# Gated linear attention in a hybrid decoder layer: the output banks are multiplied by weight and gate first, and divided by the root later and in pieces

## What is computed

```
def _head_rms(x, g):                       # per head, 128 values
    y = xf * lax.rsqrt(jnp.mean(xf * xf, axis=-1, keepdims=True) + EPS)
    return y.reshape(...) * g

oa = _gla(qa, ka, va, log_a)               # 4 heads x 128 values, 512 tokens
ya = (_head_rms(oa, gla_norm) * silu(ga)) @ w_up_a
```

```
qk = silu(_causal_dwconv(concatenate([qc, kc]), mlstm_conv))
log_f = log_sigmoid(fc + mlstm_b_f)
```

## Time and profile before

| | us |
|---|---|
| median of 3 runs (lowest, highest) | 1457.63 (1456.39, 1460.25) |
| the profiled execution: its time | 1462.21 |
| its span, from the first to the last instruction | 1460.4 |
| TensorE busy in the span | 1334.4 (91%) |
| VectorE busy | 1038.5 (71%) |
| ScalarE busy | 778.6 (53%) |
| GpSimd busy | 432.5 (30%) |
| mean granted TensorE clock | 0.948 |

### The profile page before, as it was taken

The page is one execution under the profiler, slowest core; times in us unless marked ns, Lnnn a source line. Parts: engine busy times, 40 slices in busy tenths (PEclk is TensorE's granted clock), DMA queues, the critical chain, the costliest instruction groups (busy, mean ns, idle before and its releaser), DMA issues.

```text
span 1460.4 us, 19415 instructions
## 1 busy us (share of the span) xinstructions
PE 1334.4 (91%) x6398; PEld 1023.7 (70%) x6398; DVE 1038.5 (71%) x1302; ACT 778.6 (53%) x952; POOL 432.5 (30%) x321
## 2 busy tenths in 40 slices
PE   4897888998788979998997999999999999999986
PEld 2686678665445547887974888787788888888842
DVE  1538585375798645544467898888889999998927
ACT  3613332343233443222132888888788888888811
POOL 1100010002221000000001366665656666666610
PEclk8897989889898989999998999999999999999998
DMA  9233312103023505324134999999999999999856
GB/s 300 80 102 133 116 29 87 44 15 108 20 81 130 188 15 175 107 93 159 37 130 155 330 389 412 396 384 371 341 360 387 366 350 360 359 359 358 319 214 254
DMA packets 126617, 314.57 MB, mean 215 GB/s; under 512 B 24229, under 2 KB 61418, under 8 KB 118122
## 3 DMA queue, kind: packets, MB, share of 16 engines
q1 hardware_dynamic: 108282, 288.73, 54.6%
q0 software_dynamic: 18288, 25.21, 4.8%
HBM read 316.49 MB, written 38.80 MB: 243 GB/s over the span
## 4 chain that ended last, share of the span: by engine, by line
PE 62%; DMA 13%; DVE 13%; issue 5%; ACT 4%; POOL 2%; SPq 1%; POOLq 0%; DVEq 0%; ACTq 0%
PE bank L899 15%; PE bank L1285 9%; PE bank L1313 7%; PE bank L904 7%; DMA arena<-h_dram,tok_of 6%; PE bank L1289 5%; DMA ring<-in_exp_w_up 4%; PE bank L1272 3%; DVE arena L2071 2%; DVE top L2070 2%; DMA ring<-in_w_in 1%; PE bank L1354 1%; DMA arena<-in_ada_w 1%; PE bank L846 1%; PE bank L1142 1%
## 5 line engine op out<-in xcount | busy, mean ns | idle before, releaser
L2325 DVE TENSOR_TENSOR ring_parts<-ring,arena_parts 128x2048 fp32r<-128x2048 f32 x186 | 423.2, 2289 | 59.0 <-ACT arena_parts L1670 56.5
L1670 ACT ACTIVATE arena_parts<-ring 128x2048 fp32r<-128x2048 f32 x186 | 356.0, 1930 | 41.2 <-DMA ring<-in_exp_w_up 39.7
L1285 PE MATMUL bank<-arena_parts,oTA_parts 128*128 128x512 f32 x496 | 200.0, 403 | 2.7 <-DVE oTC_parts L2341 1.5
L1285 PE MATMUL bank<-arena_parts,oTC_parts 128*128 128x512 f32 x496 | 194.7, 393 | 0.0
L1313 PE MATMUL bank<-arena_parts,oTB_parts 128*128 128x512 f32 x496 | 161.3, 407 | 5.1 <-DVE ring_parts L2325 5.1
L899 PE MATMUL bank<-hT_parts,ring_parts 128*128 128x512 f32 x344 | 145.9, 424 | 7.4 <-ACT arena L1575 3.7
L794 POOL DMA_INDIRECT y_dram<-arena,row_of x62 | 96.3, 1553 | 176.9 <-ACT arena L1697 173.8
L769 POOL DMA_INDIRECT arena<-h_dram,tok_of x61 | 129.4, 2121 | 54.5 <-POOL tok_of L781 51.0
L899 PE MATMUL bank<-x_parts,ring_parts 128*128 128x512 f32 x344 | 139.1, 404 | 0.0
L1289 PE MATMUL bank<-ring_parts,oTA_parts 128*128 128x512 f32 x496 | 133.9, 392 | 0.0
L1397 ACT ACTIVATE ring_parts<-ring 128x2048 fp32r<-128x2048 f32 (+1 forms) x38 | 64.7, 1709 | 104.6 <-DMA ring<-in_w_in 57.3
(11 more groups left out here) (421 smaller groups left out, 2299.5 us busy)
## 6 DMA issues: line engine op xcount, KB each, us to landing
ring<-in_exp_w_gate SPq DMA_DIRECT2D x124, 512.0 KB
ring<-in_exp_w_up SPq DMA_DIRECT2D x124, 512.0 KB
ring<-in_exp_w_down SPq DMA_DIRECT2D x62, 1024.0 KB
ring<-in_w_in SPq DMA_DIRECT2D x25, 1024.0 KB, 5.4
ring<-in_ada_w SPq DMA_DIRECT2D x16, 1024.0 KB, 5.8
arena<-in_ada_w SPq DMA_DIRECT2D x4, 2048.0 KB, 16.8
x<-in_x SPq DMA_DIRECT2D x2, 2048.0 KB, 12.2
ring<-in_w_o SPq DMA_DIRECT2D x4, 1024.0 KB, 5.4
```

The lines of the kernel that those rows point to most:

```text
L1285: mm(out_gu, t[c][:, tile_cols(4 * k + j)], hi[:, :, j, :], start=(k == 0 and j == 0 and x_ == 0), stop=False)
L1670: A(w_hi[c][k], w_raw[c][k], ACT.Copy).then_inc(sem("gu_hi_ready" if k < 2 else "down_hi_ready"), 1)
L2325: v.tensor_tensor(w_lo[c][k], w_raw[c][k], w_hi[c][k].bitcast(F32), ALU.subtract).then_inc(sem("gu_lo_ready" if k < 2 else "down_lo_ready" ...
```

## The change

The product by norm weight and gate is made first, straight from the bank, and gives the bank back; the division by the root is made later, in place. The roots have four buffers of their own in oT[2] in place of two in the arena (the fourth is sqA's place). GpSimd's clearing waits for the four bank reads alone. ScalarE splits w_qkc1 after the first square and w_vc0 right after the four roots, which now stand together behind the squares. VectorE divides head 0 ahead of the three copies of mb, and heads 1 to 3 behind the values of branch C.

```diff
-        rsA = [ra.take(T) for _ in range(2)]
-        hA = ra.take(T)
+        rsA = [oT[2][:, h, :] for h in range(4)]
+        ra.at += 3 * T
...
-            pool.wait_ge(sem("oTA_ready"), 4)
-            pool.wait_ge(sem("mb_ready"), 3)
+            pool.wait_ge(sem("oA_read"), 4)
             g.memset(raw, 0.0)
...
             split_hi("w_qkc0")
-            split_hi("w_qkc1")
-            for h in range(5):
-                if h < 4:
-                    b = done(act, f"oA{h}")
-                    if h:
-                        b1 = done(act, f"msA{h - 1}")
-                        if h == 3:
-                            act.wait_ge(sem("oA_read"), 1)
-                        A(rsA[(h - 1) % 2], b1[:, :], ACT.Sqrt, scale=1.0 / P,
-                          bias=epsc[:, 0:1]).then_inc(sem("root_ready"), 1)
-                    A(sqA, b[:, :], ACT.Square).then_inc(sem("squares_ready"), 1)
-                else:
-                    b = done(act, "msA3")
-                    act.wait_ge(sem("oA_read"), 2)
-                    A(rsA[1], b[:, :], ACT.Sqrt, scale=1.0 / P, bias=epsc[:, 0:1]).then_inc(sem("root_ready"), 1)
-            act.wait_ge(sem("oTA_ready"), 4)
+            for h in range(4):
+                b = done(act, f"oA{h}")
+                if h:
+                    done(act, f"msA{h - 1}")
+                A(sqA, b[:, :], ACT.Square).then_inc(sem("squares_ready"), 1)
+                if h == 0:
+                    split_hi("w_qkc1")
+            for h in range(4):
+                b = done(act, f"msA{h}")
+                A(rsA[h], b[:, :], ACT.Sqrt, scale=1.0 / P, bias=epsc[:, 0:1]).then_inc(sem("root_ready"), 1)
+            split_hi("w_vc0")
+            act.wait_ge(sem("oA_read"), 4)
             act.wait_ge(sem("fb_ready"), 1)
...
-            split_hi("w_vc0")
             split_hi("w_vc1")
...
             dve.wait_ge(sem("outgate_ready"), 5)
             for h in range(4):
+                dve.wait_ge(sem("squares_ready"), h + 1)
+                b = done(dve, f"oA{h}")
+                v.scalar_tensor_tensor(out=oT[0][:, h, :], in0=b[:, :], scalar=par[:, 26 + h:27 + h], in1=sga[:, h, :],
+                                       op0=ALU.mult, op1=ALU.mult).then_inc(sem("oA_read"), 1)
+            dve.wait_ge(sem("oA_read"), 4)
+
+            def divide_a(h):
+
                 dve.wait_ge(sem("root_ready"), h + 1)
-                if h:
-                    dve.wait_ge(sem("oTA_ready"), h)
-                link(v.reciprocal(hA, rsA[h % 2]))
-                b = done(dve, f"oA{h}")
-                v.scalar_tensor_tensor(out=hA, in0=b[:, :], scalar=par[:, 26 + h:27 + h], in1=hA, op0=ALU.mult,
-                                       op1=ALU.mult).then_inc(sem("oA_read"), 1)
-                dve.wait_ge(sem("oA_read"), h + 1)
-                v.tensor_tensor(oT[0][:, h, :], hA, sga[:, h, :], ALU.mult).then_inc(sem("oTA_ready"), 1)
-            dve.wait_ge(sem("oTA_ready"), 4)
-            for c in range(3):
-                further_columns(c)
+                link(v.reciprocal(rsA[h], rsA[h]))
+                v.tensor_tensor(oT[0][:, h, :], oT[0][:, h, :], rsA[h], ALU.mult).then_inc(sem("oTA_ready"), 1)
...
             link(v.tensor_scalar(ib, ib, bif[:, 0:1], None, ALU.add))
+            split_lo("w_vc0")
+            divide_a(0)
+            for c in range(3):
+                further_columns(c)
             dve.wait_ge(sem("cleared"), C_CLEARED)
             dve.wait_ge(sem("ln_ready"), 3)
...
                 ins.then_inc(sem("conv_ready"), 1)
-                if f >= 2:
-                    split_lo(f"w_vc{f - 2}")
+                if f == 3:
+                    split_lo("w_vc1")
...
                 split_lo(f"w_oc{q}")
+            for h in range(1, 4):
+                divide_a(h)
+            dve.wait_ge(sem("oTA_ready"), 4)
             dve.wait_ge(sem("u_ready"), 1)
```

## The result

| | before | changed |
|---|---|---|
| median, first comparison | 1457.01 us (4 runs) | 1440.49 us (4 runs, 1437.91 to 1444.38) |
| ratio, with its 95% interval | | 0.9868 (0.9824 to 0.9911) |
| median, beside the last experiments | 1457.41 us (11 runs) | 1442.96 us (6 runs) |
| ratio, with its 95% interval | | 0.9905 (0.9875 to 0.9935) |
| profiled execution: time, span | 1462.2, 1460.4 | 1441.2, 1439.3 |

1442.5 was forecast, 15.1 us less than before. VectorE is busy for as long as before: nothing was saved on it, only moved. TensorE is busy for 16 us less with the same 6398 matmuls; roughly, that is the granted clock, 0.961 on average against 0.948 (both busy times come to some 1266 us at the full clock).

What follows compares the result with a forecast made beforehand. TensorE has 62% of the chain, so VectorE counts only where TensorE waits for it. Gains of 8.3 us (earlier qk0) and 6.8 (values), with nothing for clock or divisions, take 1457.6 to 1442.5 us; range 1438 to 1448.

Steps and rivals of the forecast that it cites:

- The banks: From oA0 to qk0: squares, sums and banks finish earlier, so qk0 starts at 186.9 instead of 195.20, gaining 8.3 us.
- the first and the second term: 8.3 us from qk0 starting earlier, and 6.8 us from the values of branch C, added to 15.1 us.
- rival (b): TensorE's wait at the values stays, so only the 8.3 us at qk0 are left: 1449.3 us, chance 0.09.
- The values: From vc00 on, the wait for w_vc0's low part goes; eight values take 23.0 us instead of 29.9, gaining 6.8.
- The clock, put at nothing: At the start of the projections: TensorE's clock falls again and 2.2 us are lost again, so no gain.
- Rival (a): The clock holds from msA to the projections: 2.2 us more, 17.3 in all, 1440.3 us, chance 0.25.
- The divisions: Heads 1 to 3 on VectorE, 12.4 us in the idle 20.19 before L1972: cost nothing, 7.7 us left.
- GpSimd's clearing: Starts beside VectorE's first copy of mb; four small operations take 4 us, at worst 3 more, covered by 10.7.
- (c): The time gained is taken back later in the kernel: 1457.6 us, chance 0.05.
- (d): Slower through the next stage's clock, narrow matmuls from 275 to 350 us: 1462.9 at mean clock 0.70, chance 0.03.
- the later clock: Behind the stage: narrow matmuls shifted against the clock's falls and rises, plus or minus 3 us in every case.

Runs made afterwards that it cites:

- e1: Changed kernel with the four divisions together, the gate's rows and both parts of w_vc0 back at their old places: 1454.59 us, ratio to before 0.9982.
- e2: Changed kernel with only the early split of w_vc0 undone, both its parts at their old places: 1440.68 us, ratio to before 0.9878.
- e3: Changed kernel with all four divisions together at head 0's place, ahead of the copies of the column sums: 1440.87 us, ratio to before 0.9893.
- e4: Changed kernel with the three column sums one by one behind qk0, qk1 and qk2, copies behind the first three convolutions: 1437.14 us, ratio to before 0.9864.
- e5: Changed kernel with two further reciprocals, results unused, on VectorE behind the fourth division: 1441.47 us, ratio to before 0.9879.
- e6: Changed kernel with five further reciprocals, results unused, on VectorE behind the fourth division: 1449.56 us, ratio to before 0.9925.

## Why the prediction was right, and where not

**The banks.** Right in size and order: qk0 14.2 us after oA0, 13.9 predicted, with the one remaining wait of 0.75 us ahead of msA3 where 0.8 was worked out. The 0.3 us are the sums, 3.3 us instead of 2.9, since the clock fell within them. The order of ScalarE and VectorE was as written, and mb2 didn't wait for the roots.

**The step that failed: the first and the second term as a sum.** I added 8.3 and 6.8 as if each stood for itself, and gave rival (b), in which the wait at the values stays, the whole of the first: 1449.3. e1 shows what happens in its place. It has qk0 8.8 us earlier after oA0 than before, and the stage gains 0.6 us; the time is 1454.59 against 1458.05, an interval that includes no change. The wait at vc00, which rival (b) leaves as it was, grew from 4.82 to 9.70 us, 2.06 at uT came to it, and the low clock there cost 3.4 where it had cost 1.9. TensorE's earlier start at qk0 is a gain only while VectorE, which isn't made faster, can stay ahead of it, and the row that says so was in front of me: 4.82 us of waiting for VectorE at vc00, which an earlier TensorE would only lengthen. The number came out because the change has both parts and because the times of VectorE were worked out for the whole of it; as an account of what each part is worth, and as a price for rival (b), the sum was wrong.

**The values.** 23.2 us against 23.0. The wait of 4.82 us is gone. But I gave it to the early low part of w_vc0, and e2 shows that this part isn't needed for it: earlier sums do as well. The cover that I worked out at vc10, 7.8 us, was 8.2, and e3 confirms it by going over it.

**The clock, put at nothing.** This is the term that was mis-sized. I had taken the fall as coming again and its price as the same. It came again, but before, the clock was low for 4.2 us of qk0, and now for 5.4; the low stretch of 6.8 us begins under the sums, and I had priced it only from qk0 on. It cost 0.5 us in the sums and 2.7 from qk0 to vc00 (24.8 us against 22.1 at the full clock), 3.2 together as e4 shows, where I had put 2.2. That is about the 1.0 us by which the stage is longer than forecast. Rival (a), that the clock would hold, is refuted in both profiles of the changed kernel and in the five variants with the same order.

**The divisions** at nothing: right; L1971 had 8.2 us to spare, 7.7 predicted, and e5 and e6 bound it from both sides. **GpSimd's clearing** held VectorE's small operations, 4.4 us for the four, where 4 was taken. In e1, where they run after the clearing, the first of them takes 0.42 instead of 2.12 us; nothing waited for the difference.

**The rest.** Rival (b) did not come, and (c) and (d) did not either: behind the stage the changed kernel takes 1188.8 us and 1189.3 before. With 9 us of scatter there, the 3 us either way that I had given to the later clock can't be seen. The stage gives 14.0 us of the 15.1 forecast, the medians 16.5 and 14.5. That 1442.5 lies within 2 us of 1440.49 and within 0.5 of 1442.96 is in part luck of the runs: the stage itself came out 1.1 us short of the forecast.

## What to carry to other kernels

Freeing a buffer early helps only as far as the engine that was busy holding it is not needed again soon: before counting the gain, follow that engine's queue to the next thing that the early starter wants, for the wait may just move there. And before adding two gains, ask what each would be without the other. Work that is needed late (here three divisions, 12 us) belongs into the idle time ahead of a wait that another engine ends, and its size against that idle time says beforehand if it is free. Where two moves serve the same wait, undo each alone before believing in either.

## What the runs showed of the hardware

The granted clock of TensorE fell with TensorE busy without a gap over 0.75 us, under twelve float32 matmuls of a single column or just behind them, in seven of seven profiles, and stayed at 1.2 GHz for 6.8 us in six of them and 3.4 us in e1, into the dense products that followed. Spread in three groups of four among dense products, or ahead of oA0, the same matmuls did not bring it down in four of four; the gain was 3.2 us.

Stages that no variant touched scatter by more than I had thought: oA0 began at 164.2 to 173.0 us in the ten profiles with the same order ahead of it, and the part behind oc3 took 1183.3 to 1192.6 us. Differences of a few us are found in the stage, not in a single execution's time.
